# Expert gates of 256 tokens written by accumulating indirect DMAs instead of one-hot products

## The reference

```
q  = (t @ wq).reshape(ntok, 8, 2, 128)              # t: tokens, 1024 features
sc = einsum('thpd,hpkd->thpk', q, subkeys)          # 128 keys on each side
s1, i1 = top_k(sc[:, :, 0], 16);  s2, i2 = top_k(sc[:, :, 1], 16)
best, pos = top_k(s1[..., :, None] + s2[..., None, :], 16)
idx  = e1 * 128 + e2                                 # 8 heads x 16 experts of 16384, for each token
gate = softmax(best)
act  = gelu(u_tab[idx] . t) * gate                   # u_tab, v_tab: 16384 x 1024
out  = sum_k act_k * v_tab[idx_k]
```

## Time and profile before

| | us |
|---|---|
| median of 3 runs | 3638.95 (3638.54 to 3649.3) |
| profiled execution | 3639.07 |
| its span | 3637.2 |
| PE busy in the span | 3538.1 |
| VectorE busy | 2284.6 |
| ScalarE busy | 1472.4 |
| GpSimd busy | 884.6 |

### The profile page before, as it was taken

How to read it: one execution, slowest core, us unless ns; L and a number is a source line. 1 busy time by engine, 2 the same in 40 slices (tenths; PEclk the granted TensorE clock), 3 DMA queues, 4 the chain that set the end, 5 groups by cost and what they waited for, 6 DMA issues and landing times.

```text
span 3637.2 us, 56094 instructions
## 1 busy us (share of the span) xinstructions
PE 3538.1 (97%) x22572; PEld 3247.0 (89%) x22572; DVE 2284.6 (63%) x3965; ACT 1472.4 (40%) x2191; POOL 884.6 (24%) x795
## 2 busy tenths in 40 slices
PE   8999999999899999999998999999999999999998
PEld 8988999999797678788677877899999999999998
DVE  7445465554844545555687444479988885777775
ACT  7254453222625435222466444243333433333333
POOL 4010022111401012211213201035646662111110
PEclk9999999999999999999999999999999999999999
DMA  4212232222221123222222122348869999999894
GB/s 155 70 42 65 76 116 93 93 92 94 70 65 54 63 82 133 95 97 93 75 81 70 60 93 81 95 140 272 281 214 258 298 289 338 314 310 313 307 312 139
DMA packets 293617, 544.70 MB, mean 150 GB/s; under 512 B 138288, under 2 KB 187568, under 8 KB 292976
## 3 DMA queue, kind: packets, MB, share of 16 engines
q1 hardware_dynamic: 185248, 394.34, 32.6%
q0 software_dynamic: 27648, 100.68, 8.4%
q10 hardware_dynamic: 80464, 46.10, 4.3%
HBM read 483.67 MB, written 56.62 MB: 149 GB/s over the span
## 4 chain that ended last, share of the span: by engine, by line
PE 86%; DVE 8%; ACT 3%; issue 1%; POOL 1%; DMA 0%; ACTq 0%; DVEq 0%; POOLq 0%
PE PSM L317 19%; PE PSM L318 18%; PE PSM L319 18%; PE PSM L211 5%; PE PSM L3160 5%; PE PSM L3162 5%; PE PSM L3161 5%; PE PSM L3136 3%; DVE PARTS L284 2%; ACT PARTS L275 1%; PE PSM L1061 1%; DVE MH L1741 1%; PE PSM L825 1%; PE PSM L1097 1%; DVE QK L1375 1%
## 5 line engine op out<-in xcount | busy, mean ns | idle before, releaser
L284 DVE TENSOR_TENSOR PARTS<-RAW,PARTS 128x1024 fp32r<-128x1024 f32 (+1 forms) x612 | 743.8, 1220 | 476.4 <-ACT PARTS L275 476.2
L275 ACT ACTIVATE PARTS<-RAW 128x1024 fp32r<-128x1024 f32 x612 | 645.4, 1057 | 932.1 <-PE PSM L319 488.6
L317 PE MATMUL PSM<-UX,PARTS 128*128 128x264 f32 (+3 forms) x2912 | 987.1, 339 | 27.4 <-DVE UX L2297 4.9
L318 PE MATMUL PSM<-UX,PARTS 128*128 128x264 f32 (+3 forms) x2912 | 970.2, 333 | 0.0
L319 PE MATMUL PSM<-UX,PARTS 128*128 128x264 f32 (+3 forms) x2912 | 969.5, 333 | 0.0
L317 PEld LDWEIGHTS PSM<-UX,PARTS 128*128 128x128 f32 x2912 | 548.8, 188 | 78.4 <-issue 9.2
L318 PEld LDWEIGHTS PSM<-UX,PARTS 128*128 128x128 f32 x2912 | 549.0, 189 | 29.9 <-issue 1.7
L319 PEld LDWEIGHTS PSM<-UX,PARTS 128*128 128x128 f32 x2912 | 547.9, 188 | 29.7
L3160 PE MATMUL PSM<-AC,PARTS 128*128 128x416 f32 x1024 | 358.3, 350 | 2.3 <-DVE AC L3457 2.3
L3162 PE MATMUL PSM<-AC,PARTS 128*128 128x416 f32 x1024 | 357.6, 349 | 0.0
L3161 PE MATMUL PSM<-AC,PARTS 128*128 128x416 f32 x1024 | 357.5, 349 | 0.0
(11 more groups left out here) (516 smaller groups left out, 5815.9 us busy)
## 6 DMA issues: line engine op xcount, KB each, us to landing
RAW<-w_ff_dram SPq DMA_DIRECT2D x128, 512.0 KB, 3.2
RAW<-peer_u_dram SPq DMA_DIRECT2D x128, 512.0 KB, 4.8
RAW<-peer_v_dram SPq DMA_DIRECT2D x128, 512.0 KB, 5.1
RAW<-w_in_dram SPq DMA_DIRECT2D x116, 512.0 KB, 3.2
acts_dram<-MQ ACTq DMA_DIRECT2D x128, 208.0 KB, 4.2
MQ<-acts_dram SPq DMA_DIRECT2D x128, 208.0 KB, 3.8
MQ<-gates_dram SPq DMA_DIRECT2D x128, 208.0 KB, 4.7
RAW<-w_mix_o_dram SPq DMA_DIRECT2D x32, 512.0 KB, 3.3
```

What stands on the lines that cost most here:

```text
L275: e.activation(p[:, 0:1024], self.raw.of(i), ACT.Copy).then_inc(S.sem, S.tick("w", i))
L284: e.tensor_tensor(p[:, 1024:1024 + n], r[:, 0:n], p[:, 0:n].bitcast(F), SUB).then_inc(V.sem, V.tick("w", i))
L317: e.matmul(dst, wh[k], xh_[k][:, lo:hi], start=(k == 0), stop=False, skip_group_check=True)
L318: e.matmul(dst, wh[k], xl_[k][:, lo:hi], start=False, stop=False, skip_group_check=True)
```

## The change

For tokens 0 to 255 (tiles 0 and 1) no gates are built by products. Instead:

- `Gd[:, :, 0:256]` is cleared in the second layer's feed-forward: GpSimd fills a tile of zeros, ScalarE's queue issues 8 DMAs that write 16.8 MB.
- `placed(n)`: VectorE works out for each token and slot the position in `Gd` (in step 34 and step 52) and copies the gates aside, six small operations for tile 0 and four for tile 1.
- `scatter(n, s_)`: GpSimd issues one indirect DMA for each slot, 128 elements of 4 bytes, one for each token, with an accumulating write. `scatters_by` spreads the 256 over steps: 66 in steps 36 to 68, 54 in steps 69 to 89, 136 in steps 90 to 124. Before every sixteenth of a tile GpSimd waits until all earlier ones of the tile have landed.
- `FILLS` has three fills left (tokens 384 to 415 and 256 to 383), in steps 70 to 89; `turn` is left out for tiles 0 and 1.
- 26 of the 96 row products of the few tokens (`THERE = 70`) move with their gathers from the first phase to steps 6 to 29 of the second, ahead of the 96 sums, and share the 8 buffers with them; ScalarE's Gelu over the products moves to step 29.
- SP waits before the first `back` for all writes of the gates and all scatters.

```
-        FILLS = [(3, 384, 4)] + [(g // 2, 64 * g, 8) for g in range(6)]
-        FILL_AT = [70] + [74 + 8 * g for g in range(6)]
+        FILLS = [(3, 384, 4)] + [(g // 2, 64 * g, 8) for g in range(4, 6)]
+        FILL_AT = [70, 74, 82]
+        Gflat = Gd.rearrange("n p t -> (n p t)").unsqueeze(1)
+        place_ = [qb(oE1 + 128 * n, 128).bitcast(U32) for n in range(2)]
+        share_ = [qb(oGt + 128 * n, 128) for n in range(2)]
...
+                if l == 1 and g < 8:
+                    if g == 0:
+                        e.wait_ge(G.sem, G.at("zeros"))
+                    src = zeros.unsqueeze(1).to_broadcast([128, 16, SCATTERED])
+                    e.dma_start(Gd[16 * g:16 * g + 16, :, 0:SCATTERED].rearrange("n p t -> p n t"), src).then_inc(zero_out, 16)
...
+        def scatters_by(i):
+            for i0, i1, q0, q1 in ((36, 69, 0, 66), (69, 90, 66, 120), (90, 125, 120, 256)):
+                if i0 <= i < i1:
+                    return q0 + (q1 - q0) * (i + 1 - i0) // (i1 - i0)
+            return 0 if i < 36 else 256
...
                 if j == 0:
-                    e.wait_ge(g_out[0], 16 * 48)
-                if j % 8 == 0 and j < 64:
-                    e.wait_ge(g_last[j // 8], 16)
-                elif j == 64:
-                    e.wait_ge(g_out[1], 16 * 56)
+                    e.wait_ge(g_out[0], 16 * 16)
+                    e.wait_ge(g_out[1], 16 * 32)
+                    for placed in placed_out:
+                        e.wait_ge(placed, 16 * 128)
...
+        LATE = FEW - THERE
+        WHOLE = 6 + 114 * LATE // (FEW + LATE - 1)
+
+        def late_at(i):
+            return [r for r in range(FEW + LATE) if i == 6 + 114 * r // (FEW + LATE - 1)]
...
+            def placed(n):
+                e1, e2, gv = chosen_[n]
+                if n == 0:
+                    e.scalar_tensor_tensor(out=spot, in0=con["ident"], scalar=1.0, in1=iota, op0=MUL, op1=MUL,
+                                           accum_out=column[:, 0:1]).then_inc(V.sem, V.tick())
+                    e.wait_ge(V.sem, V.n)
+                    e.tensor_scalar(column[:, 1:2], column[:, 0:1], 128.0, None, ADD).then_inc(V.sem, V.tick())
+                e.tensor_copy(share_[n], gv).then_inc(V.sem, V.tick())
+                e.scalar_tensor_tensor(out=spot, in0=e2, scalar=128.0, in1=e1, op0=MUL, op1=ADD).then_inc(V.sem, V.tick())
+                e.wait_ge(V.sem, V.n)
+                e.scalar_tensor_tensor(out=spot, in0=spot, scalar=float(TD), in1=column[:, n:n + 1].to_broadcast([128, 128]),
+                                       op0=MUL, op1=ADD).then_inc(V.sem, V.tick())
+                e.wait_ge(V.sem, V.n)
+                e.tensor_copy(place_[n], spot).then_inc(V.sem, V.tick("placed", n))
...
+            def scatter(n, s_):
+                if s_ == 0:
+                    e.wait_ge(V.sem, V.at("placed", n))
+                    e.wait_ge(zero_out, 16 * 8)
+                elif s_ % 16 == 0:
+                    e.wait_ge(placed_out[n], 16 * s_)
+                e.indirect_dma_start(Gflat, bass.IndirectOffsetOnAxis(ap=place_[n][:, s_:s_ + 1], axis=0),
+                                     share_[n][:, s_:s_ + 1], None, compute_op=ADD).then_inc(placed_out[n], 16)
...
                 for n, t8 in gates_at(i):
                     one_hots(n, t8)
-            e.wait_ge(g_out[0], 16 * 48)
-            for s_ in range(FEW):
-                if s_ >= 8:
-                    e.wait_ge(V.sem, V.at("sum", s_ - 8))
+                for n, s_ in scatters_at(i):
+                    scatter(n, s_)
+            e.wait_ge(g_out[0], 16 * 16)
+            for r in range(FEW + LATE):
+                if r >= LATE + 8:
+                    e.wait_ge(V.sem, V.at("sum", r - LATE - 8))
+                elif r >= 8:
+                    e.wait_ge(V.sem, V.at("dot", THERE + r - 8))
```

More of the change, by code:

```diff
@@ L152, in program @@
         g_out = [sem(f"g_out{i}") for i in range(2)]
-        g_last = [sem(f"g_last{i}") for i in range(8)]
+        zero_out = sem("zero_out")
+        placed_out = [sem(f"placed_out{i}") for i in range(2)]
         few_in = sem("few_in")
@@ L1675, in ff_pool @@
             n = TT - 16 * l
+            if l == 1:
+                e.memset(zeros, 0.0).then_inc(G.sem, G.tick("zeros"))
             for i in range(32):
@@ L1756, in program @@
         c2 = {n: sb(oC2 + o, w) for n, (o, w) in C2_OFF.items()}
+        SCATTERED = 256
+        zeros = sb(oT + 5120, SCATTERED)
         four = lambda o: [sb(o + i * 512, 512) for i in range(4)]
@@ L2943, in program @@
         chosen_ = [[CH[:, 384 * n + 128 * i:384 * n + 128 * i + 128] for i in range(3)] for n in range(4)]
-        sm = qb(place(16), 16)
+        sm = qb(place(32), 32)
         TD, FEW, HALVES = 416, 96, 64
@@ L3002, in turn_at, with placed_at, scatters_at, late @@
         def turn_at(i):
-            return [n for c, n in enumerate(ORDER) if i == 18 * c + 18]
+            return [n for c, n in enumerate(ORDER) if i == 18 * c + 18 and n >= 2]
+        def placed_at(i):
+            return [n for c, n in enumerate(ORDER) if i == 18 * c + 16 and n < 2]
+        def scatters_by(i):
[3 more added lines that the diff above has]
+            return 0 if i < 36 else 256
+        def scatters_at(i):
+            return [(q // 128, q % 128) for q in range(scatters_by(i - 1), scatters_by(i))]
         def dots_at(i):
-            return [s_ for s_ in range(FEW) if i == dot_at(s_)]
+            return [s_ for s_ in range(THERE) if i == dot_at(s_)]
         def dot_at(s_):
-            return 21 + 45 * s_ // (HERE - 1) if s_ < HERE else 77 + 49 * (s_ - HERE) // (FEW - 1 - HERE)
+            return 21 + 45 * s_ // (HERE - 1) if s_ < HERE else 77 + 49 * (s_ - HERE) // (THERE - 1 - HERE)
         def rows(s_):
-            return (gu[s_ % 5], gu_in[s_ % 5], s_ // 5 + 1) if s_ < HERE else (
-                gu2[s_ % 3], gu_in[5 + s_ % 3], (s_ - HERE) // 3 + 1)
+            if s_ < HERE:
+                return gu[s_ % 5], gu_in[s_ % 5], s_ // 5 + 1
+            if s_ < THERE:
+                return gu2[s_ % 3], gu_in[5 + s_ % 3], (s_ - HERE) // 3 + 1
+            return late(s_ - THERE)
+        def late(r):
+            return gv_[r % 8], gv_in[r % 8], r // 8 + 1
         def gathers_at(i):
-            return [s_ for s_ in range(FEW) if i == (
+            return [s_ for s_ in range(THERE) if i == (
                 (18 if s_ < 5 else dot_at(s_ - 5) + 1) if s_ < HERE else (75 if s_ < HERE + 3 else dot_at(s_ - 3) + 1))]
-        def sums_at(i):
-            return [s_ for s_ in range(FEW) if i == 6 + 114 * s_ // 95]
+        LATE = FEW - THERE
+        WHOLE = 6 + 114 * LATE // (FEW + LATE - 1)
+        def late_at(i):
+            return [r for r in range(FEW + LATE) if i == 6 + 114 * r // (FEW + LATE - 1)]
         def group(s_):
@@ L3037, in out_sp @@
         def out_sp(i):
-            return [(f, c) for f in range(7) for c in range(8) if i == last_at(f) + 5 + 3 * c // 4]
+            return [(f, c) for f in range(3) for c in range(8) if i == last_at(f) + 5 + 3 * c // 4]
         def out_act(i):
-            return [(f, c) for f in range(7) for c in range(8, 16) if i == last_at(f) + 1 + 3 * (c - 8) // 4]
+            return [(f, c) for f in range(3) for c in range(8, 16) if i == last_at(f) + 1 + 3 * (c - 8) // 4]
         def half_of(f):
@@ L3070, in peer_sp @@
                     e.wait_ge(S.sem, S.at("gates", f, FILLS[f][2] - 1))
-                    e.dma_start(*gates_out(f, c)).then_inc(g_last[c] if f == 6 else g_out[half_of(f)], 16)
+                    e.dma_start(*gates_out(f, c)).then_inc(g_out[half_of(f)], 16)
                 if i >= NB:
@@ L3263, in peer_act @@
             store(NB - 1)
-            e.wait_ge(V.sem, V.at("dot", FEW - 1))
-            for a, _, _ in few:
-                e.activation(a, a, ACT.Gelu_apprx_tanh).then_inc(S.sem, S.tick("few"))
             for i in range(NB):
@@ L3271, in peer_act @@
                     rounded(i + 1)
+                if i == WHOLE - 1:
+                    e.wait_ge(V.sem, V.at("dot", FEW - 1))
+                    for a, _, _ in few:
+                        e.activation(a, a, ACT.Gelu_apprx_tanh).then_inc(S.sem, S.tick("few"))
             for d in range(8):
@@ L3417, in sum_ @@
                 w, c = group(s_)
-                x, a, y = gv_[s_ % 8], few[w][0][:, c:c + 1], few_y[w]
-                e.wait_ge(gv_in[s_ % 8], 16 * (s_ // 8 + 1))
+                x, landed, turn_ = late(LATE + s_)
+                a, y = few[w][0][:, c:c + 1], few_y[w]
+                e.wait_ge(landed, 16 * turn_)
                 if s_ == 0:
-                    e.wait_ge(g_out[1], 16 * 56)
-                    for done in g_last:
-                        e.wait_ge(done, 16)
+                    e.wait_ge(g_out[1], 16 * 32)
                 if c == 0:
@@ L3441, in peer_dve @@
                     share(n)
+                for n in placed_at(i):
+                    e.wait_ge(V.sem, V.n)
+                    placed(n)
```

(24 more changed lines are left out.)

4 lines of the change are left out of this document (3 added, 1 removed).

## The result

The changed kernel takes 3862.14 us in the median of its runs (3858.92 to 3868.63); the kernel before took 3641.86 beside it. The ratio is 1.0597 (95% interval 1.0583 to 1.061): slower by some 220 us. The profiled execution has a span of 3866.8 us; it is the slowest of the four (3868.63), so that times read from its trace come out up to 6.5 us longer than the median.

The account below looks back on a forecast made before the run. PE bounds the kernel before, but GpSimd's queue takes over: 172.3 kept work + 355.6 scatters + 42 waits + 9.4 start the second phase 75 us later. 3637.2 + 75 + 1.9 = 3714 us, range 3595 to 3870.

Parts of the forecast that it names:

- the 57 us: First phase, PE: 32 blocks of 16 matmuls removed at 1.78 us each, 57.0 us, the whole possible gain.
- The three ways to PE: First phase: PE held back by line 290, then GpSimd's one-hots, then VectorE waiting for gathers in its products.
- the price of the scatter: GpSimd before the second phase: 256 scatters priced like gathers with 0.30 us of issue, 355.6 us.
- The bound from above, 2.24: GpSimd: upper bound of 2.24 us per scatter, from the distance of three gathers, 4.48 / 2.
- start of the stretch: First phase: scatters begin in step 36, its end placed at 2540, 504.3 us before the second phase.
- waits for earlier scatters: GpSimd: 14 waits, one before every sixteenth scatter, about 3.0 us of idle queue each, 42 us.
- from there to the second phase: End of first phase: landing 3.0, load of gates 4.7, then product, rounding and rest at 0.58 each: 9.4 us.
- If VectorE slows GpSimd more than the means say: First phase: a condition, without a size, under which the forecast would be wrong.
- Hidden parts: Clearing, moved row products and their gathers: each counted 0; at worst 16 us for clearing, 40 us for the gathers.
- Cheap: Rival, GpSimd: each scatter takes 0.94 us without the 0.30; second phase 40 us earlier, 3599 us; chance 0.28.
- Dear: Rival, GpSimd: adding or DMA queues make each scatter 2.24 us; 293 us later, 3932 us; chance 0.20.
- The DMA-bound second phase: Rival, second phase: scatters fit but DMA bounds it; -57 and up to +40 us, or -17; chance 0.05.

Follow-up runs that it names:

- e1: Changed kernel without the 256 scatters and the wait for them (gates of 256 tokens stay zero): 3591.63 us, ratio 0.9845.
- e6: Changed kernel with the same 256 adding scatters, but none before step 69: 3912.43 us, ratio 1.0727.
- e10: Changed kernel with all one-hots on VectorE and none on GpSimd: 3818.05 us, ratio 1.0466.
- e2: Changed kernel with scatters that write instead of adding: 3728.62 us, ratio 1.0222.
- e3: Kernel before with the clearing of 16.8 MB alone: 3646.21 us, ratio 0.9993.
- e4: Kernel before with the move of 26 row products and their gathers alone: 3642.46 us, ratio 0.9994.

## Why the prediction missed

**The direction and the mechanism held.** I had put GpSimd's single queue in the place of PE, and it is there: next to nothing in it waits but for its own scatters, e1 without scatters gives 55.5 of the 57 us back, e6 loses about what is left unused of it, e10 gains most of what is taken out of it. The three ways to PE came in the forecast order.

**The step that failed is the price of the scatter**, "66 x (1.23 + 0.30) = 101.0; the other 190 x (1.04 + 0.30) = 254.6. Sum 355.6". I priced an adding scatter by gathers. Measured: 431.4 + 71.8 us of issue = 503.2, or 1.97 each, 147.6 us more. That is, within 1 us, the whole distance between the forecast start of the second phase and the measured one (3119.3 and 3267.5), but that is luck: the other terms missed by up to 22 us each, and cancel. And e2 shows that it is the addition: plain scatters cost 282.2 + 69.3 = 351.5 us, 4 from my term, and that kernel takes 3728.62 where I had forecast 3714. The bound from above, 2.24, did hold the value, but I took the price from rows of gathers, none of which adds, and gave the addition no term of its own.

The other terms, between the first scatter and the second phase:

| term | predicted us | measured us |
|---|---|---|
| start of the stretch | at 2540.0 | at 2555.1 |
| scatters and their issue | 355.6 | 503.2 |
| waits for earlier scatters | 42 | 25.0 |
| line 290 (291) | 41.8 | 53.7 |
| one-hots | 65.8 | 68.2 |
| gathers and their gaps | 64.7 | 71.8 |
| other idle, overlap of records | 0 | -21.9 |
| from there to the second phase | 9.4 | 12.4 |
| the second phase starts | 3119.3 | 3267.5 |

The overlap is what makes the terms add up to the 700.0 us of the stretch; 22.5 of it are the 28 subtractions and 13 one-hots behind a scatter.

**The start of the stretch.** I placed the end of step 36 at 2540, and that reading is one step off. GpSimd works three blocks ahead and shares the subtraction up to block 67, so its last one is that of step 64; of the 29 after 2540 the first, at 2540.97, is step 36's own, and the step ends with its gather, near 2543.4. The remaining 11.5 us are the distance between the two traces (the same subtraction stands at 2552.43 in the changed kernel); they are of the size by which executions of one kernel differ, and no cause is shown for them.

**The waits.** I took 3.0 us for each of 14; nine show in the trace, 25.0 us in all, 1.69 to 3.54 each with a mean of 2.8, and a landing 3.1 us after the issue in the median. The five that are not seen had a subtraction and a gather (three) or one-hots (two) between them and the scatter before. So the length of a wait was near my number, and the count was not. The Trainium skill (DMA: Bandwidth & Descriptors, the anatomy of one DMA) gives 2.0 us of fixed cost, by which my estimate had been 28 us for all 14. The sum in the trace is nearer to that than to 42, but by the count: the mean of those that show is 2.8 us.

**The end.** I had 9.4 us from the last scatter to the second phase; it took 12.4, and the path is another one. In SP's queue loads of weights stand behind its wait for all scatters as well, and the first of them, with its rounding and subtraction ahead of the product with the gates, is on the path. From the chain that ended last, without the short pieces:

```profile
3253.60 3.02 DMA gates_dram<-MQ
3257.57 5.32 DMA RAW<-peer_v_dram
3262.91 1.06 ACT PARTS L276
3263.99 1.23 DVE PARTS L285
```

**Neighbours.** "If VectorE slows GpSimd more than the means say" did not come true. The means that I took for plain scatters, 1.23 and 1.04, give 1.09 over all 256, and in e2 they last 1.10. The weight subtraction seems slower, 1.92 us in the mean instead of 1.44, but its record overlaps that of the adding scatter ahead of it by 0.55 us, all 28 times, and from the scatter's end on it takes 1.36. Two rows of GpSimd's timeline in the changed kernel, then two in e2, where nothing overlaps and the mean is 1.39:

```profile
2573.49 1.57 POOL L3573 DMA_INDIRECT gates_dram<-MQ  x1 [0.30 <-issue]
2574.50 1.87 POOL L291 TENSOR_TENSOR PARTS<-RAW,PARTS 128x512 fp32r<-128x512 f32 x1
```

```profile
2573.60 0.97 POOL L3573 DMA_INDIRECT gates_dram<-MQ  x1 [0.30 <-issue]
2574.60 1.29 POOL L291 TENSOR_TENSOR PARTS<-RAW,PARTS 128x512 fp32r<-128x512 f32 x1
```

What makes some of the adding scatters longer than 1.54 us is not shown; all of it together is 431.4 - 256 x 1.54 = 37 us.

**Hidden parts.** The clearing and the moved rows were counted at 0, and e3 and e4 measure 0. The second phase was counted at 0 more too. It lasts 584 us in the changed kernel, 577 in e4 with the same transfers in it, 578 in e2 and 582 in e1, but 583 in e3 as well, whose second phase is that of the kernel before (578 us). So the moved rows are not the cause, and it is no wait of PE, which is busy 582.46 of 583 us there; what makes these few us was not settled.

**The rivals.** "Cheap" is out: even a plain scatter keeps the 0.30. "Dear" was at 3932, 70 us above what came, and one of its reasons, an addition that costs more, is right, but at 1.97 and not 2.24. Its other reason, transfers that hold GpSimd back, is not seen: the DMA share is 0.56 at 3000 to 3100 while the scatters go out 1.84 us apart. The estimate of 3870 by the Trainium skill (DMA: Bandwidth & Descriptors, rules for kernel authors), which wants small transfers coalesced, came out near, but for another reason. Between the waits the DMAs are not held back by each other: they land 3.1 us after their issue and go out every 1.84 us. What counts here is the issuing engine's time for each. The DMA-bound second phase is out: in e1 PE is busy for 581.6 of its 582 us.

## What to carry to other kernels

Ask of each new instruction not only which engine has idle time but how much of that engine's queue is left up to the next stage, with the issue gaps, and do the sum before choosing how many to move, for each stretch by itself: here 256 did not fit and cost 220 us, 128 did and gained 14 us where some stood in the fullest stretch and 25 us where none did. An operation that is in no row wants to be run once by itself; a variant of it, as an adding DMA of a gather, is not its price. Small scatters are charged for the most part by the instruction, so the busy time of the engine in the page, 77 of 100 us here, says little about how full its queue is.

## What the runs showed of the hardware

- An indirect DMA that adds 128 elements of 4 bytes holds GpSimd for 1.54 us at least (median 1.56, mean 1.69), one that writes them for 0.95 (0.97, 1.10), and between two in a row there are 0.30 us. With 64 offsets the adding one takes 1.40 at least (median 1.42): most of it is fixed.
- The adding one moves its elements in 144 packets, the plain one in 32, and a gather of 128 rows in 144 as well. With 64 offsets the adding one has 80 ((48128 - 27648) / 256).
- The record of the work behind an adding scatter starts some 0.55 us before the scatter's record ends (41 times, e.g. at 2574.50), but that work is not done sooner: a subtraction that takes 1.29 us by itself ends 1.3 us after the scatter's end. So means of such work look longer than they are.
- Clearing 16.8 MB in 8 DMAs beside a stage in which PE is full cost nothing that could be measured (ratio 0.9993).
- Where PE waited in many short pieces, its granted clock was lower: 0.83 in 3000 to 3100 with PE busy for 72 of 100 us, and 0.79 over 2670 to 3300 in e6, busy for 371 of 630, so a part of each stretch ran at the lower of its two levels, 1.2 GHz. It did not set the time there, as the queue of GpSimd, which next to never waited for PE, did.
